# Decay exponents of a state-space scan built by differences between heads, and a root refinement moved to GpSimd

## The chip, the cores and the metric

The kernel runs on one core of a Trainium2 chip. The metric is the device time of one execution in microseconds. Before the change it is 1761.82 us, the median of 3 runs (1761.11 to 1761.87).

## The reference

Two transformer blocks over 512 positions of width 1024 are computed in float32. The change is in the second block's second mixer, a bidirectional state-space scan (`ssd_mixer`) with 32 heads of 64 channels in 4 groups of 8 heads, 4 chunks of 128 positions, and a state of 128. Cut to what matters:

```python
cs = jnp.cumsum(aa, axis=1)                          # log decay, per head
seg = cs[:, :, None] - cs[:, None, :]
decay = jnp.exp(jnp.where(mask, seg, -jnp.inf))      # 128 x 128 per chunk, head and direction
qk = jnp.einsum('bjgn,blgn->bjlg', qq, kk)           # shared by the 8 heads of a group
y_intra = jnp.einsum('bjlgh,blghp->bjghp', qk[..., None] * decay, vv)
...
y = y.reshape(bsz, s, SSD_INNER) * jax.nn.silu(z)
yg = y.reshape(bsz, s, SSD_GROUPS, SSD_INNER // SSD_GROUPS)
yg = yg * lax.rsqrt(jnp.mean(yg * yg, axis=-1, keepdims=True) + EPS)
```

## The kernel before, in words

Features lie on the partitions, positions along the free dimension. Large products are made in three passes of fp32r parts (`three`, L387 to L389: high by high, low by high, high by low). The weights come by DMA through a ring of five slots; ScalarE makes their high part (L342), VectorE the low part (L349).

The scan (`ssd_pe`, `ssd_act`, `ssd_dve`, `ssd_pool`) runs over four groups g of eight heads, and each engine's program is an order written out by hand, with semaphores between them. After a state part (`turn_x`, `states`, `between`), a group has 16 **steps** n, one for each head and direction. The four head pairs i of a group, the two heads hh of a pair and the two directions d make up n.

- `spread` on TensorE (L2309, L2310) fills one bank of PSUM (4 or 5, by n % 2) with two matmuls: the mask (`veil`, -1e30 where the mask is off) through the identity, and the running decay sums `cst_t` of one head, picked by a column of `sel` and broadcast to all rows. It waits until the exponentials of step n-2 have read the bank (`e_x`).
- `decays` on ScalarE (L2436) takes the exponential of the bank in four pieces of 128 columns, with a bias for each chunk, into one of four buffers `em`. It waits for `spread` (`xp`) and for the consumer of the buffer (`intra`).
- `weigh` on VectorE (L2582) multiplies the buffer by the products `gmat`, from SBUF into SBUF.
- `inside` on TensorE (L2327) multiplies two weighed buffers (both heads of the pair, one direction) into the output bank. There are eight of it in a group, m = 0 to 7, 16 matmuls of 128 columns each in pairs of column groups.
- `carried` (L2318) adds what comes from the states, once for each pair.
- `evac_y` on VectorE (L2587) takes the finished pair out of PSUM after steps 5, 9, 13 and after 15. GpSimd then gates it (L2514), from SBUF into SBUF.

Before the change, step n stands for pair n // 4, direction n % 4 // 2, head n % 2. So `inside` of index m reads steps 2m and 2m+1.

Between the steps TensorE does parts of the projection z (`part_z`, 6 matmuls of 512 columns a part). In the last group it has none, and does parts of the output projection instead (`out3_step`). ScalarE also does `gates` (two table loads and four Silu, L2442 to L2445), ahead of the steps in groups 0 to 2 and before step 4 in group 3, further the high part of a weight slot after step 8, the logarithm and exponential for the roots of group g-1 after step 1 (L2418, L2420). In group 3 it also makes high parts of the output (L2424).

VectorE finishes the roots of group g-1 in groups 1 to 3: `root_half` after step 4 (L2600), three refining operations after steps 5, 6 and 7 (L2605, L2608, L2612), and `normed_y` after steps 9 to 12 (L2616). After step 11 stand a low part of a weight slot and `take_z` (L349, L2570; not in group 3), and in group 3 low parts of the output (L2635).

The order on TensorE within a group is, for m = 0 to 7: `spread` of steps 2m+2 and 2m+3, `carried` if m is even, `part_z` if m is odd, `inside`. In group 3 come `out3_step` for the tiles k = 0, 1, 2 after m = 1 (18 matmuls) and more of them after m = 4 to 7.

Of the kernel before, what the change touches and what calls it, by code (L numbers as in the profile page):

```python
# [12 lines left out]
P = 128  # L13
D = 1024
S = 512
# [152 lines left out]
def build(nc, dr, ctx, start):  # L168
# [61 lines left out]
    vtl = at("vtl", [P, 2, GW], ST + 95)  # L230
    btok = at("btok", [P, TT, NS], ST + 99)
    nrm_a = at("nrm_a", [P, S], ST + 101)
    em = at("em", [P, 4, S], 56)
    sel = at("sel", [P, 2 * SH], 102.75, F32R)
    aneg = at("aneg", [P, 2 * SH], 102.5)
    cv = at("cv", [P, 4, S], ST + 8)
    cs_tmp = at("cs_tmp", [P, S], ST + 16, F32R)
# [1845 lines left out]
        return buf[:, :, :, :].rearrange("p c d h -> p (c d h)")  # L2083

    def step_of(n):
        return n // 4, n % 2, n % 4 // 2

    def swept(s, d):
        return s if d == 0 else TT - 1 - s
# [155 lines left out]
    def ssd_pe(pe):  # L2245
# [56 lines left out]
        def spread(g, n):  # L2302
            i, hh, d = step_of(n)
            if n < 2:
                pe.wait_ge(xtc, TT * (g + 1))
            else:
                pe.wait_ge(e_x, STEPS * g + n - 1)
            col = SH * d + HPG * g + 2 * i + hh
            nc.tensor.matmul(bank[4 + n % 2][:, :], ident_r[:, :], veil[:, d:d + 1, :].to_broadcast([P, TT, P]), start=True, stop=False)  # L2309
            nc.tensor.matmul(bank[4 + n % 2][:, :], sel[:, col:col + 1].to_broadcast([P, P]), cst_t[:, :], start=False, stop=True).then_inc(xp, 1)  # L2310

        def carried(g, i):
            if i < 2:
# [6 lines left out]

        def inside(g, m):
            i, d = m // 2, m % 2
            pe.wait_ge(mlu, STEPS * g + 2 * m + 2)
            for c in range(TT):
                for hh in range(2):
                    n = 2 * m + hh
                    mm = nc.tensor.matmul(bank[2 + i % 2][hh * HD:(hh + 1) * HD, c * P:(c + 1) * P],  # L2327
                                          xtok[:, c, (2 * i + hh) * HD:(2 * i + hh + 1) * HD], em[:, n % 4, c * P:(c + 1) * P],
                                          start=False, stop=d == 1 and c == TT - 1, skip_group_check=True)
            mm.then_inc(intra, 1)  # L2330

# [6 lines left out]
            for q in range(4):  # L2338
                part_z(t, q)
        pe.wait_ge(xsilu, 24)  # L2340
        pe.wait_ge(sel_done, 2)
        begin(0)
        for g in range(SG):
            turn_x(g)
            part_z(4 * g + 2, 0)
            states(g, 0)
            part_z(4 * g + 2, 1)
            part_z(4 * g + 2, 2)
            between(g, 0)
            part_z(4 * g + 2, 3)  # L2350
            states(g, 1)
            part_z(4 * g + 3, 0)
            part_z(4 * g + 3, 1)
            between(g, 1)
            part_z(4 * g + 3, 2)
            states(g, 2)
            part_z(4 * g + 3, 3)
            spread(g, 0)
            spread(g, 1)
            between(g, 2)  # L2360
            if g:
                norm_sum(g - 1)
            if g + 1 < SG:
                for q in range(4):
                    part_z(4 * g + 4, q)
            for m in range(8):
                if m < 7:
                    spread(g, 2 * m + 2)
                    spread(g, 2 * m + 3)
                else:  # L2370
                    if g + 1 < SG:
                        begin(g + 1)
                if m % 2 == 0:
                    carried(g, m // 2)
                if m % 2 and g + 1 < SG:
                    part_z(4 * g + 5, m // 2)
                inside(g, m)
                if g == SG - 1:
                    for k in ((), (0, 1, 2), (), (), (3,), (4,), (5, 6), (7,))[m]:
                        out3_step(pe, 0, k)  # L2380
                        out3_step(pe, 1, k)
# [44 lines left out]
    def ssd_act(act):  # L2426
        z0 = PLAN["z"]["slot0"]

        def decays(g, n):
            i, hh, d = step_of(n)  # L2430
            h = HPG * g + 2 * i + hh
            act.wait_ge(xp, STEPS * g + n + 1)
            if n >= 4:
                act.wait_ge(intra, 8 * g + n // 2 - 1)
            for c in range(TT):
                e = nc.scalar.activation(em[:, n % 4, c * P:(c + 1) * P], bank[4 + n % 2][:, c * P:(c + 1) * P], ACT.Exp,  # L2436
                                         bias=lbias[:, c, d, h:h + 1])
            e.then_inc(e_x, 1)

# [60 lines left out]
    def ssd_pool(pool):  # L2500
        pool.wait_ge(dt_ok, 1)
        pool.wait_ge(tri_load, 16)
        for d, m in enumerate(("gt", "le")):
            nc.gpsimd.tensor_scalar(veil[:, d, :], M[m], NEG, None, ALU.mult)
        nc.gpsimd.tensor_copy(ident_r[:, :], C["ident"]).then_inc(sel_done, 1)
        for g in range(SG):
            if g:
                for i in range(1, 4):
                    add_squares(pool, g - 1, i)
            for i in range(4):  # L2510
                k = 4 * g + i
                pool.wait_ge(yev, k + 1)
                pool.wait_ge(zs_done, k + 1)
                nc.gpsimd.tensor_tensor(xbc[:, k, :], xbc[:, k, :], zt[:, i, :], ALU.mult).then_inc(gated, 1)  # L2514
        for i in range(1, 4):
            add_squares(pool, SG - 1, i)

    def add_squares(pool, g, i):
        pool.wait_ge(ysq, 4 * g + i + 1)
# [4 lines left out]
    def ssd_dve(dve):  # L2524
# [53 lines left out]
        def weigh(g, n):  # L2578
            dve.wait_ge(e_x, STEPS * g + n + 1)
            if n == 0:  # L2580
                dve.wait_ge(gl_done, g + 1)
            nc.vector.tensor_tensor(em[:, n % 4, :], em[:, n % 4, :], gmat[:, :], ALU.mult).then_inc(mlu, 1)  # L2582

        def evac_y(g, i):
            k = 4 * g + i
# [12 lines left out]
        def root_half(g):  # L2598
            dve.wait_ge(yln, 2 * g + 1)
            nc.vector.tensor_scalar(nrm_a[:, :], bank[6][:, :], -0.5 / GW, -0.5 * EPS, ALU.mult, ALU.add).then_inc(yhalf, 1)  # L2600

        def root_first(g):
            dve.wait_ge(yhalf, g + 1)
            dve.wait_ge(yln, 2 * g + 2)
            link("dve", dve, nc.vector.tensor_tensor(xbc[:, C_TILE + g, :], nrm_a[:, :], xbc[:, B_TILE + g, :], ALU.mult))  # L2605

        def root_second(g):
            link("dve", dve, nc.vector.tensor_tensor(xbc[:, C_TILE + g, :], xbc[:, C_TILE + g, :], xbc[:, B_TILE + g, :], ALU.mult))  # L2608

        def root_third(g):  # L2610
            r = xbc[:, B_TILE + g, :]
            link("dve", dve, nc.vector.scalar_tensor_tensor(out=r, in0=xbc[:, C_TILE + g, :], scalar=1.5, in1=r, op0=ALU.add, op1=ALU.mult))  # L2612

        def normed_y(g, i):
            k = 4 * g + i
# [23 lines left out]
        for g in range(SG):  # L2639
# [13 lines left out]
            for n in range(STEPS):  # L2653
# [2 lines left out]
                    evac_y(g, n // 4 - 1)  # L2656
                if n == 4 and g:
                    root_half(g - 1)
                if n == 5 and g:
                    root_first(g - 1)  # L2660
                if n == 6 and g:
                    root_second(g - 1)
                if n == 7 and g:
                    root_third(g - 1)
                if 9 <= n < 13 and g:
                    normed_y(g - 1, n - 9)
                if n == 11 and g + 1 < SG:
# [48 lines left out]
    def _(pool):  # L2716
# [3 lines left out]
        nc.gpsimd.memset(half_eps[:, :], -0.5 * EPS).then_inc(set_done, 1)  # L2720
        pool.wait_ge(cst_load, 16)
        nc.gpsimd.tensor_tensor(sel[:, :], C["ident"][:, 0:2 * SH], C["ident"][:, 2 * SH:P], ALU.add).then_inc(sel_done, 1)
        one_pool(pool)
        two_pool(pool)
        up_pool(pool, 0)
# [243 lines left out]
```

## Time and profile before

| quantity | value |
|---|---|
| median of 3 runs | 1761.82 us |
| the profiled execution's own time | 1761.53 us |
| its span | 1759.8 us |
| TensorE (PE) busy | 1729.4 us, 98% |
| VectorE (DVE) busy | 1170.9 us, 67% |
| ScalarE (ACT) busy | 790.3 us, 45% |
| GpSimd (POOL) busy | 182.0 us, 10% |
| granted TensorE clock | 1.00 |
| the scan's steps | about 1092 to 1302 us |

Busy shares are of the whole span, and the scan is an eighth of it. In the timeline a row is one instruction or several merged: start, time from its start to its end, engine, line, operation, out<-in, how often. The bracket gives the idle time of the engine before it and what ended that. Ends overlap the next start, since the engines pipeline: the distance between starts is what an instruction occupies.

### The profile page before, as it was taken

How to read it: one execution, taken by the hardware profiler on the slowest of the kernel's cores; microseconds unless marked ns; L12 is line 12 of the kernel's file. 1: busy time of each engine (PE TensorE's matmuls, PEld its weight loads, DVE VectorE, ACT ScalarE, POOL GpSimd, SP SyncE). 2: the span in 40 equal slices, each digit the busy share in tenths (PEclk: the TensorE clock that was granted, in tenths of full speed). 3: DMA queues.
4: the chain of work that ended last, by engine and by line, in shares of the span. 5: the costliest groups of instructions: out<-in, count | busy, mean ns of one | idle time of the engine just before them, and what ended most of it. 6: DMA issues, size and time to landing. Idle time of an engine off the chain costs nothing.

```text
span 1759.8 us, 21732 instructions
## 1 busy us (share of the span) xinstructions
PE 1729.4 (98%) x8630; PEld 1380.5 (78%) x8630; DVE 1170.9 (67%) x1653; ACT 790.3 (45%) x1364; POOL 182.0 (10%) x203
## 2 busy tenths in 40 slices
PE   9999999999999999999999999999989999999998
PEld 7887877776578888888897886777668888888887
DVE  5565774867668887663368996766684688766334
ACT  5565652642244544442244544475562445444221
POOL 0421001400000111110000000221120001111000
PEclk9999999999999999999999999999999999999999
DMA  6211123311122222233323221011112132222332
GB/s 222 96 61 59 62 96 122 95 58 60 60 72 91 93 99 100 96 91 104 92 68 114 84 99 57 25 37 37 37 49 96 48 132 96 96 96 93 99 96 72
DMA packets 44277, 147.95 MB, mean 84 GB/s; under 512 B 5264, under 2 KB 8464, under 8 KB 44048
## 3 DMA queue, kind: packets, MB, share of 16 engines
q1 hardware_dynamic: 41728, 141.89, 24.3%
q10 hardware_dynamic: 2448, 4.66, 0.9%
q8 instruction: 69, 1.13, 0.3%
q14 instruction: 32, 0.26, 0.1%
HBM read 144.44 MB, written 2.10 MB: 83 GB/s over the span
## 4 chain that ended last, share of the span: by engine, by line
PE 82%; DVE 12%; ACT 4%; issue 1%; DMA 1%; POOL 1%; ACTq 0%; DVEq 0%; POOLq 0%
PE bank L387 21%; PE bank L389 21%; PE bank L388 21%; DVE cv L2226 4%; DVE w_lo L349 2%; PE bank L404 2%; PE bank L406 2%; PE bank L405 2%; PE bank L2327 1%; PE bank L2288 1%; PE bank L2300 1%; PE bank L983 1%; PE bank L996 1%; DVE bank L813 1%; PE bank L2309 1%
## 5 line engine op out<-in xcount | busy, mean ns | idle before, releaser
L387 PE MATMUL bank<-a_hi,w_hi 128*128 128x512 f32 x1384 | 555.2, 401 | 2.7 <-DVE a_lo L1270 1.1
L349 DVE TENSOR_TENSOR w_lo<-raw,w_hi 128x1024 fp32r<-128x1024 f32 (+1 forms) x257 | 328.2, 1282 | 335.6 <-ACT w_hi L342 335.0
L389 PE MATMUL bank<-a_hi,w_lo 128*128 128x512 f32 x1384 | 539.3, 390 | 0.0
L388 PE MATMUL bank<-a_lo,w_hi 128*128 128x512 f32 x1384 | 539.0, 389 | 0.0
L342 ACT ACTIVATE w_hi<-raw 128x1024 fp32r<-128x1024 f32 (+1 forms) x259 | 268.1, 1042 | 307.0 <-DMA raw<-in_w_down 143.5
L387 PEld LDWEIGHTS bank<-a_hi,w_hi 128*128 128x128 f32 x1384 | 259.8, 188 | 77.1 <-issue 20.3
L388 PEld LDWEIGHTS bank<-a_lo,w_hi 128*128 128x128 f32 x1384 | 259.9, 188 | 58.9 <-issue 6.9
L389 PEld LDWEIGHTS bank<-a_hi,w_lo 128*128 128x128 f32 x1384 | 259.8, 188 | 55.1
L1357 ACT ACTIVATE u<-bank,par 128x512 f32<-128x512 f32 x88 | 68.6, 779 | 177.8 <-DVE bank L813 177.8
L387 PE MATMUL bank<-g_hi,w_hi 128*128 128x512 f32 x308 | 119.8, 389 | 0.0
L388 PE MATMUL bank<-g_lo,w_hi 128*128 128x512 f32 x308 | 119.8, 389 | 0.0
L389 PE MATMUL bank<-g_hi,w_lo 128*128 128x512 f32 x308 | 119.8, 389 | 0.0
L1400 POOL TENSOR_TENSOR gv<-u 128x512 f32<-128x512 f32 x44 | 57.4, 1304 | 557.3 <-DVE u L1376 557.3
L2436 ACT ACTIVATE em<-bank,lbias 128x128 f32<-128x128 f32 x256 | 70.8, 392 | 33.7 <-PE bank L2310 33.4
L2582 DVE TENSOR_TENSOR em<-em,gmat 128x512 f32<-128x512 f32 x64 | 49.9, 787 | 38.6 <-ACT em L2436 38.4
L2226 DVE SCALAR_TENSOR_TENSOR cv<-bank,par,cv 128x510 f32<-128x510 f32 (+1 forms) x96 | 71.7, 747 | 2.5
L1376 DVE SCALAR_TENSOR_TENSOR u<-bank,par,u 128x511 f32<-128x511 f32 x88 | 66.0, 750 | 3.1
L389 PEld LDWEIGHTS bank<-g_hi,w_lo 128*128 128x128 f32 x308 | 57.8, 188 | 12.0
L388 PEld LDWEIGHTS bank<-g_lo,w_hi 128*128 128x128 f32 x308 | 57.8, 188 | 12.0
L387 PEld LDWEIGHTS bank<-g_hi,w_hi 128*128 128x128 f32 x308 | 57.8, 188 | 12.0
L404 PE MATMUL bank<-a_hi,w_hi 128*128 128x256 f32 (+1 forms) x192 | 61.1, 318 | 4.7 <-DVE w_lo L774 2.5
L1373 DVE SCALAR_TENSOR_TENSOR u<-bank,par,u 128x511 f32<-128x511 f32 x88 | 65.0, 739 | 0.0
(398 smaller groups left out, 2543.4 us busy)
## 6 DMA issues: line engine op xcount, KB each, us to landing
raw<-in_w_up SPq DMA_DIRECT2D x88, 512.0 KB, 3.2
raw<-in_w_in SPq DMA_DIRECT2D x50, 512.0 KB, 3.2
raw<-in_w_out SPq DMA_DIRECT2D x32, 512.0 KB, 3.7
raw<-in_w_down SPq DMA_DIRECT2D x32, 512.0 KB, 3.5
raw<-in_w_xbc SPq DMA_DIRECT2D x24, 512.0 KB, 3.2
raw<-in_w_z SPq DMA_DIRECT2D x16, 512.0 KB, 3.2
raw<-in_w_down SPq DMA_DIRECT2D x16, 384.0 KB, 3.1
raw<-in_w_mem_kv SPq DMA_DIRECT2D x4, 512.0 KB, 3.2
```

The source lines that it names most:

```text
L342: nc.scalar.activation(w_hi[:, q % RING, 0:w], raw[:, q % RING, 0:w], ACT.Copy).then_inc(hi_done, 1)
L349: nc.vector.tensor_tensor(w_lo[:, q % RING, 0:w], raw[:, q % RING, 0:w], w_hi[:, q % RING, 0:w].bitcast(F32), ALU.subtract).then_inc(lo_do ...
L387: nc.tensor.matmul(out, wh, rhs_hi[:, k, :], start=k == first, stop=False)
L388: nc.tensor.matmul(out, wh, rhs_lo[:, k, :], start=False, stop=False)
L389: return nc.tensor.matmul(out, wl, rhs_hi[:, k, :], start=False, stop=stop)
L404: nc.tensor.matmul(out, wh, rhs_hi[:, k, cols], start=start, stop=False, skip_group_check=True)
L1357: nc.scalar.activation(u[:, t % 4, :], tile_bank(name, t)[:, :], ACT.Identity, scale=pcol(f"ffn_w{layer}", 3 * t + 1), bias=pcol(f"ffn_b{l ...
L1373: nc.vector.scalar_tensor_tensor(out=ut[:, 1:S], in0=pt_[:, 0:S - 1], scalar=pcol(w, 3 * t), in1=ut[:, 1:S], op0=ALU.mult, op1=ALU.add).th ...
L1376: nc.vector.scalar_tensor_tensor(out=ut[:, 0:S - 1], in0=pt_[:, 1:S], scalar=pcol(w, 3 * t + 2), in1=ut[:, 0:S - 1], op0=ALU.mult, op1=ALU ...
L1400: nc.gpsimd.tensor_tensor(gv[:, i % 2, :], u[:, 2 * i % 4, :], u[:, 2 * i % 4 + 1, :], ALU.mult).then_inc(prod, 1)
L2226: nc.vector.scalar_tensor_tensor(out=dst, in0=tile_bank("xbc", tile)[:, a + by:b + by], scalar=pcol("conv_w", 5 * tile + tap), in1=dst, op ...
L2436: e = nc.scalar.activation(em[:, n % 4, c * P:(c + 1) * P], bank[4 + n % 2][:, c * P:(c + 1) * P], ACT.Exp, bias=lbias[:, c, d, h:h + 1])
```

## The change

It does two things. First, a step's exponents are made from those of the step before in the same bank. A bank belongs to one direction now. The mask is written once for each group and direction (n < 2), and each later step adds a matmul whose selecting column is the difference between this head's column and the preceding head's (`seld`), on top of what the bank holds. For this the steps are renumbered: pair n // 4, head n % 4 // 2, direction n % 2. `inside` of index m = 2i + d then reads steps 4i + d and 4i + 2 + d, there are five buffers `em` instead of four, and the order of TensorE is written anew. Second, the three refining operations leave VectorE for four on GpSimd, behind `add_squares` and ahead of the gating of the group's first pair. VectorE waits for them before `normed_y`, after step 9.

```diff
-    em = at("em", [P, 4, S], 56)
+    em = [at(f"em{n}", [P, S], kb) for n, kb in enumerate((56, 58, 60, 62, ST + 80))]
+    seld = at("seld", [P, 2 * SG, HPG], 103, F32R)
@@ step_of
-        return n // 4, n % 2, n % 4 // 2
+        return n // 4, n % 4 // 2, n % 2
@@ spread
-            col = SH * d + HPG * g + 2 * i + hh
-            nc.tensor.matmul(bank[4 + n % 2][:, :], ident_r[:, :], veil[:, d:d + 1, :].to_broadcast([P, TT, P]), start=True, stop=False)
-            nc.tensor.matmul(bank[4 + n % 2][:, :], sel[:, col:col + 1].to_broadcast([P, P]), cst_t[:, :], start=False, stop=True).then_inc(xp, 1)
+            if n < 2:
+                nc.tensor.matmul(bank[4 + d][:, :], ident_r[:, :], veil[:, d:d + 1, :].to_broadcast([P, TT, P]),
+                                 start=True, stop=False, skip_group_check=True)
+            nc.tensor.matmul(bank[4 + d][:, :], seld[:, SG * d + g, 2 * i + hh:2 * i + hh + 1].to_broadcast([P, P]), cst_t[:, :],
+                             start=False, stop=True, skip_group_check=True).then_inc(xp, 1)
@@ inside
-            pe.wait_ge(mlu, STEPS * g + 2 * m + 2)
+            pe.wait_ge(mlu, STEPS * g + 4 * i + 3 + d)
-                    n = 2 * m + hh
+                    n = 4 * i + 2 * hh + d
@@ the order of TensorE
+            spread(g, 2)
+            spread(g, 3)
+            carried(g, 0)
             for m in range(8):
-                if m < 7:
-                    spread(g, 2 * m + 2)
-                    spread(g, 2 * m + 3)
-                else:
-                    if g + 1 < SG:
-                        begin(g + 1)
-                if m % 2 == 0:
-                    carried(g, m // 2)
-                if m % 2 and g + 1 < SG:
-                    part_z(4 * g + 5, m // 2)
+                i, d = m // 2, m % 2
+                if m < 6:
+                    spread(g, 4 * i + 4 + 2 * d)
+                elif d and g + 1 < SG:
+                    begin(g + 1)
                 inside(g, m)
+                if m < 6:
+                    spread(g, 4 * i + 5 + 2 * d)
+                if d == 0 and g + 1 < SG:
+                    part_z(4 * g + 5, i)
+                if d and i < 3:
+                    carried(g, i + 1)
@@ decays
-            if n >= 4:
-                act.wait_ge(intra, 8 * g + n // 2 - 1)
+            if n >= 5:
+                act.wait_ge(intra, 8 * g + 2 * ((n - 5) // 4) + (n - 5) % 2 + 1)
@@ ssd_pool, in groups 1 to 3 after add_squares
+                refine_pool(pool, g - 1)
+    def refine_pool(pool, g):
+        a, r, t = nrm_a[:, :], xbc[:, B_TILE + g, :], xbc[:, C_TILE + g, :]
+        pool.wait_ge(yhalf, g + 1)
+        pool.wait_ge(yln, 2 * g + 2)
+        link("pool", pool, nc.gpsimd.tensor_tensor(t, a, r, ALU.mult))
+        link("pool", pool, nc.gpsimd.tensor_tensor(t, t, r, ALU.mult))
+        link("pool", pool, nc.gpsimd.tensor_scalar(t, t, 1.5, None, ALU.add))
+        link("pool", pool, nc.gpsimd.tensor_tensor(r, r, t, ALU.mult))
+        root_made.append(count["pool"])
@@ ssd_dve
-                if n == 5 and g:
-                    root_first(g - 1)
-                if n == 6 and g:
-                    root_second(g - 1)
-                if n == 7 and g:
-                    root_third(g - 1)
+                if n == 9 and g:
+                    dve.wait_ge(chain["pool"], root_made[g - 1])
@@ gpsimd, at the start of the program
+        pool.wait_ge(sel_done, 1)
+        heads_of = sel[:, :].rearrange("p (n h) -> p n h", h=HPG)
+        nc.gpsimd.tensor_copy(seld[:, :, 0:1], heads_of[:, :, 0:1])
+        nc.gpsimd.tensor_tensor(seld[:, :, 1:HPG], heads_of[:, :, 1:HPG].bitcast(F32), heads_of[:, :, 0:HPG - 1].bitcast(F32),
+                                ALU.subtract).then_inc(sel_done, 1)
```

## Rows read from the trace of the kernel before

**Rows 1.** The page: busy time of each engine, share of the span, instructions.

```profile
PE 1729.4 (98%) x8630; PEld 1380.5 (78%) x8630; DVE 1170.9 (67%) x1653; ACT 790.3 (45%) x1364; POOL 182.0 (10%) x203
```

**Rows 2.** Windows, steps of groups 0, 1, 3: PE, PEld, DVE, ACT, POOL busy, clock, DMA.

```profile
1096.00:1120.70 24.70, 24.70 (x214) 19.72 (x213) 14.33 (x19) 15.90 (x53) 3.82 (x3) 1.00 0.01 3
1153.80:1180.00 26.20, 25.16 (x216) 19.79 (x215) 19.49 (x28) 17.24 (x58) 5.63 (x3) 1.00 0.05 17
...
1266.60:1301.60 35.00, 29.07 (x221) 21.49 (x219) 27.19 (x37) 27.86 (x77) 6.87 (x3) 1.00 0.00 1
```

**Rows 3.** Timeline of TensorE in group 0.

```profile
1102.64 1.09 PE L2327 MATMUL bank<-em,xtok 128*64 128x128 f32 x16
1103.66 0.50 PE L2309 MATMUL bank<-veil,ident_r 128*128 128x512 f32 x1
1104.00 0.39 PE L2310 MATMUL bank<-cst_t,sel 128*128 128x512 f32 x1
1104.23 0.39 PE L2309 MATMUL bank<-veil,ident_r 128*128 128x512 f32 x1
...
1109.19 1.09 PE L2327 MATMUL bank<-em,xtok 128*64 128x128 f32 x16
```

**Rows 4.** Timeline of ScalarE, VectorE and GpSimd in group 0.

```profile
1107.94 2.17 ACT L2436 ACTIVATE em<-bank,lbias 128x128 f32<-128x128 f32 x8 [0.39 <-PE bank L2310]
1108.19 0.74 DVE L2587 SCALAR_TENSOR_TENSOR xbc<-xbc,par,bank 128x512 f32<-128x512 f32 x1
1109.01 1.27 POOL L2514 TENSOR_TENSOR xbc<-xbc,zt 128x512 f32<-128x512 f32 x1 [6.18 <-DVE xbc L2587]
1109.11 2.31 DVE L2582 TENSOR_TENSOR em<-em,gmat 128x512 f32<-128x512 f32 x2 [0.18 <-ACT em L2436]
```

**Rows 5.** Timeline in group 1, all engines.

```profile
1153.35 4.46 ACT L2436 ACTIVATE em<-bank,lbias 128x128 f32<-128x128 f32 x16
1153.85 1.09 PE L2327 MATMUL bank<-em,xtok 128*64 128x128 f32 x16
...
1157.43 0.68 DVE L2600 TENSOR_SCALAR nrm_a<-bank 128x512 f32<-128x512 f32 x1
...
1165.62 0.69 DVE L2582 TENSOR_TENSOR em<-em,gmat 128x512 f32<-128x512 f32 x1 [1.17 <-ACT em L2436]
...
1174.90 1.09 PE L2327 MATMUL bank<-em,xtok 128*64 128x128 f32 x16 [1.04 <-DVE em L2582]
1175.43 1.28 DVE L2582 TENSOR_TENSOR em<-em,gmat 128x512 f32<-128x512 f32 x2
```

**Rows 6.** Timeline in group 3, all engines.

```profile
1269.95 1.28 ACT L2442 ACT_TABLE_LOAD   x1
1270.19 1.09 PE L2327 MATMUL bank<-em,xtok 128*64 128x128 f32 x16
...
1274.75 1.14 ACT L2436 ACTIVATE em<-bank,lbias 128x128 f32<-128x128 f32 x4
...
1280.84 1.25 ACT L2436 ACTIVATE em<-bank,lbias 128x128 f32<-128x128 f32 x4
...
1286.55 0.68 DVE L2582 TENSOR_TENSOR em<-em,gmat 128x512 f32<-128x512 f32 x1
...
1296.53 2.88 POOL L2514 TENSOR_TENSOR xbc<-xbc,zt 128x512 f32<-128x512 f32 x1 [6.22 <-DVE xbc L2587]
1296.54 1.09 PE L2327 MATMUL bank<-em,xtok 128*64 128x128 f32 x16
1296.97 0.68 DVE L2582 TENSOR_TENSOR em<-em,gmat 128x512 f32<-128x512 f32 x1
```

**Rows 7.** Groups by line on GpSimd.

```profile
L2522 POOL TENSOR_TENSOR xbc<-xbc 128x512 f32<-128x512 f32 x12 | 15.4, 1284 | 14.9 <-ACT xbc L2414 14.9
L2504 POOL TENSOR_SCALAR veil<-tri 128x128 fp32r<-128x128 f32 x2 | 2.0, 985 | 171.9 <-DVE da L2162 171.8
L2718 POOL MEMSET spin<- 128x512 f32 x1 | 0.5, 524 | 0.0
```

More of the change, by code:

```diff
@@ L2322, in inside @@
             i, d = m // 2, m % 2
-            pe.wait_ge(mlu, STEPS * g + 2 * m + 2)
+            pe.wait_ge(mlu, STEPS * g + 4 * i + 3 + d)
             for c in range(TT):
                 for hh in range(2):
-                    n = 2 * m + hh
+                    n = 4 * i + 2 * hh + d
                     mm = nc.tensor.matmul(bank[2 + i % 2][hh * HD:(hh + 1) * HD, c * P:(c + 1) * P],
-                                          xtok[:, c, (2 * i + hh) * HD:(2 * i + hh + 1) * HD], em[:, n % 4, c * P:(c + 1) * P],
+                                          xtok[:, c, (2 * i + hh) * HD:(2 * i + hh + 1) * HD], em[n % 5][:, c * P:(c + 1) * P],
                                           start=False, stop=d == 1 and c == TT - 1, skip_group_check=True)
@@ L2340, in ssd_pe @@
         pe.wait_ge(xsilu, 24)
-        pe.wait_ge(sel_done, 2)
+        pe.wait_ge(sel_done, 3)
         begin(0)
@@ L2432, in decays @@
             act.wait_ge(xp, STEPS * g + n + 1)
-            if n >= 4:
-                act.wait_ge(intra, 8 * g + n // 2 - 1)
+            if n >= 5:
+                act.wait_ge(intra, 8 * g + 2 * ((n - 5) // 4) + (n - 5) % 2 + 1)
             for c in range(TT):
-                e = nc.scalar.activation(em[:, n % 4, c * P:(c + 1) * P], bank[4 + n % 2][:, c * P:(c + 1) * P], ACT.Exp,
+                e = nc.scalar.activation(em[n % 5][:, c * P:(c + 1) * P], bank[4 + n % 2][:, c * P:(c + 1) * P], ACT.Exp,
                                          bias=lbias[:, c, d, h:h + 1])
@@ L2516, in ssd_pool @@
             add_squares(pool, SG - 1, i)
+    root_made = []
+    def refine_pool(pool, g):
[7 more added lines that the diff above has]
+        root_made.append(count["pool"])
     def add_squares(pool, g, i):
@@ L2581, in weigh @@
                 dve.wait_ge(gl_done, g + 1)
-            nc.vector.tensor_tensor(em[:, n % 4, :], em[:, n % 4, :], gmat[:, :], ALU.mult).then_inc(mlu, 1)
+            nc.vector.tensor_tensor(em[n % 5][:, :], em[n % 5][:, :], gmat[:, :], ALU.mult).then_inc(mlu, 1)
         def evac_y(g, i):
@@ L2600, in root_half @@
             nc.vector.tensor_scalar(nrm_a[:, :], bank[6][:, :], -0.5 / GW, -0.5 * EPS, ALU.mult, ALU.add).then_inc(yhalf, 1)
[L2602 to L2612, printed above, removed]
         def normed_y(g, i):
```

## The prediction, made before the change was timed

> **What bounds the kernel now.** The busy times come first [rows 1]: TensorE is busy 98% of the span. A TensorE instruction taken away should then be worth its own time, wherever TensorE does not wait. The windows over the steps of the four groups say where that holds [rows 2]. In group 0 TensorE is busy all 24.7 us and no other engine over 16. In group 1 it is idle 1.0 of 26.2 us, with VectorE at 19.5 (group 2 is the same pattern once more, 59.1 us later). In group 3 it is idle 6 of 35 us, with VectorE and ScalarE at 27 to 28. So the gain is plain only in group 0. There the timeline [rows 3] shows what a matmul occupies: starts 0.23 us apart, though each lasts 0.39.
>
> An average doesn't show the dependences, so I then followed one pair of heads in the timelines of all engines. A step needs exponentials, 8 pieces in 2.17 us [rows 4], so 1.14 us until one step's are done and 1.03 between two; a weighing, 0.69 us [rows 5]; then `inside`, which occupies 1.02 us (from 1102.64 to 1103.66 [rows 3]). Before, `inside` m needs steps 2m and 2m+1, which are let go by `inside` m-2 or earlier, so spreads, `carried` or z hide this latency. A pair takes 6.55 us (from 1102.64 to 1109.19 [rows 3]), set by TensorE's order.
>
> **TensorE's gain.** Of 64 mask matmuls 8 stay. 56 x 0.23 = **12.9 us** less to issue, or 0.92 us a pair, half of what the spreads cost.
>
> **The new dependence.** `inside` of even index 2i+2 now needs step 4i+6 instead of 4i+5. That step's exponentials wait for `inside` 2i+1, which frees their buffer (five buffers: step 6 takes that of step 1). Before, nobody needed the step after it so soon. Set t = 0 at the end of `inside` 2i+1 and go on in group 0:
> - `evac_y` of the pair runs on VectorE to 0.8, and GpSimd starts gating at 0.85. Gating lasts 1.27 us, to 2.1.
> - The exponentials of step 4i+6 run from 0.1 to 1.25. The weighing is ready then but does not run: two weighings that began beside a gating took 2.31 us instead of 1.28 [rows 4, 5], so VectorE stood still until GpSimd was through. It runs from 2.1 to 2.8.
> - TensorE has only spread, `carried` and spread for this time, 1.4 us. It then idles 1.4 us until 2.8.
> - `inside`, spread, six z matmuls, spread with the small gaps after a wait, and the next `inside` add 1.02 + 0.23 + 1.38 + 0.30 + 1.02 = 3.95.
>
> The pair takes 2.8 + 3.95 = **6.75 us** and not 6.55: the latency costs more than the removed matmuls gave. Three such pairs add 0.6 to 0.9 us (0.85 with the ends of the waits), and the first `inside` starts 0.2 later, at the end of weighing 2. Group 0: **+1.0 us**.
>
> **Groups 1 and 2.** The first `inside` needs the weighing of step 2, whose exponentials start at 1153.35 behind the roots' logarithm and exponential [rows 5]. 1153.35 + 1.14 + 0.03 + 0.69 = 1155.2, against 1153.85 now: +1.4. The removed masks only pay this back. Two further terms count, both on VectorE:
> - **Refinement.** The three VectorE operations free 3 x 0.69 = 2.1 us, but GpSimd's four take the port from VectorE's weighings. A product takes GpSimd 1.28 us [rows 7]. For the 512-column scalar add the trace has no row: above it lies such a product (1.28), below it a memset of that size (0.52) [rows 7]. A scalar operation of a quarter of the columns took 0.985 us there, so I take 1.0. The block is 3 x 1.28 + 1.0 + links of 0.07 = 5.1 us. It starts at 1158.1, behind `root_half` (1157.43 + 0.68 [rows 5]); VectorE and GpSimd then alternate. Weighings 5, 6, 7 and 8 each wait for one operation of it. 1158.1 + 5.1 + 4 x 0.6 puts the end of weighing 8 at 1165.6. Then GpSimd gates the first pair, late, for 1.27. If it is first, weighing 9 starts at 1166.9, if VectorE is first, at 1165.6, where it starts now (1165.62 [rows 5]). A gating that lasted 2.88 us [rows 6] had been passed by more than one VectorE operation, so either occurs; nearer the upper end, since the gating then hits a later operation: **+1.0**.
> - **One weighing more.** From weighing 9 on VectorE is the bound: with evacuation, four normings, a weight's low part and z, it works without a gap from 1165.62 to the end of weighing 13, and `inside` 6 starts right behind that at 1174.90 [rows 5]. `inside` 6 now needs weighing 14, behind the evacuation at 0.66 and its own 0.6: +1.3.
>
> Together +2.3 a group, twice (group 2 repeats group 1). The block's own wait, before step 9's first norming, costs nothing: it ends before weighing 9. The sum for both is **+4.6 us**.
>
> GpSimd is said to be nearly as fast as VectorE for one-input elementwise work by the Trainium skill (GPSIMD Engine Reference, "Engine selection"); an estimate for the scalar add by that would be about 0.7 us, and each group then 0.3 us less. No row here has that operation at that size.
>
> **Group 3.** ScalarE does its gates ahead of step 4, 1269.95 to 1274.75 [rows 6]. Now TensorE fills that hole with `inside` 1 at 1270.19 [rows 6] and the 18 output matmuls right behind it. After the change `spread` 6, which waits for the exponentials of step 4 (1274.75 + 1.14 = 1275.9), stands **ahead of** `inside` 1. So `inside` 1, spread, `carried` and the 18 matmuls (1.02 + 0.3 + 0.95 + 4.14 = 6.4 us) start only at 1276.2 and end at 1282.6. Then comes `spread` 8, so step 8's exponentials start at 1283.1 and not at 1280.84 [rows 6]: +2.3. From there the chain of ScalarE and VectorE is as now, and weighing 9 moves from 1286.55 to 1288.85 [rows 6]. `inside` 6 again needs weighing 14, which now ends 1296.97 + 0.68 = 1297.65, 1.1 us behind the start of `inside` 6 at 1296.54 [rows 6]. That gives +3.4. Weighing 14 can also meet the gating of the third pair, 0 to +1.27, of which I take half: **+4.0 us**. What follows (gating, squares, sums, output projection) hangs on it and moves along.
>
> **The rest.** Two more GpSimd operations at the start (about 1 us each by [rows 7]) lie beside a time when nothing waits for GpSimd; were that cover gone they would cost 2 us. One z part moves from odd to even m, same length; no DMA is moved.
>
> **Sum.** 1.0 + 4.6 + 4.0 = +9.6 us. The profiled execution took 1761.5 us and its span 1759.8, so the next should have a span of about 1769.4 and a time of 1771.1. The median of the runs stands 0.3 us above the profiled execution: **1771.4 us**.
>
> **Rivals.**
> - *The saving comes through.* The mechanism is that the wait ahead of even `inside` stays below 0.92 us a pair, as it does if gating doesn't hold the weighing and GpSimd's refinement runs beside VectorE. For it: TensorE has no idle time in group 0 [rows 2]. Against: the 2.31 us [rows 4]. If all of it held, 1761.8 - 12.9 = 1748.9; with the latency alone (a pair of 1.25 + 0.7 + 3.95 = 5.9 instead of 6.55) and nothing of VectorE's bound, 9 pairs x 0.65 = 5.9 less: 1756.
> - *Even.* Gating and weighing collide in part only: group 0 gains 1.0, groups 1 and 2 stay, group 3 loses about 1.2 by `spread` 6. That is 1762.
> - *The port costs more.* Each GpSimd operation is lengthened by VectorE's as well, the scalar add takes 2 us, and normings then wait for the block. +2 us for each of three groups: 1777.4. For it: the gating of 2.88 us [rows 6].
> - *It doesn't do what it says.* Excluded for the matmuls, whose count is fixed in the code; if the roots came wrong nothing in time would change.
>
> The rule that decides between the first two is stated in the Trainium skill (SBUF — State Buffer, "SBUF: two separate sides"): VectorE operations with two SBUF inputs and GpSimd exclude each other for a whole instruction. By that rule, the trace agrees (2.31 us for two weighings).
>
> **How the numbers follow.** Forecast 0.70; the port costs more 0.08; even 0.09; the saving comes through 0.13. Its own range is 1767.5 to 1775: the scalar add (-1.4 to +0.8), the first gatings (-2 to +0.4), the gating in group 3 (0.6 either way), and a pair in group 0 between 6.5 and 6.9 us. For 8 in 10 I reach down toward even and up toward the dearer port: 1765.5 to 1777. A measurement tells about 0.2%, 3.5 us. Slower 0.79, same 0.09, faster 0.12.
>
> **What would show it.** In the profile after: mask matmuls x8; in groups 0 to 2, TensorE idle before even `inside`, ended by the weighing; weighings of 1.8 us or so next to GpSimd; in group 3 an idle stretch of about 5 us on TensorE before `spread` 6, and output matmuls only after 1277. If VectorE shows no long weighings, or the starts of `inside` in group 0 lie under 6 us apart by pairs, I am wrong.

## The result, and the profile after

| | median, us | lowest to highest | runs |
|---|---|---|---|
| before | 1761.59 | 1761.11 to 1761.87 | 4 |
| after | 1771.84 | 1770.33 to 1773.40 | 4 |

The ratio is 1.0059, 95% interval 1.0045 to 1.0073: the changed kernel is 10.2 us slower, though it issues 56 matmuls less. The page of the changed kernel, whose first lines answer to [rows 1]:

```profile
span 1770.4 us, 21612 instructions
## 1 busy us (share of the span) xinstructions
PE 1722.1 (97%) x8574; PEld 1373.8 (78%) x8574; DVE 1169.3 (66%) x1644; ACT 790.3 (45%) x1364; POOL 202.4 (11%) x217
```

TensorE is busy 7.3 us less over a span that is 10.6 us longer. So it stands idle 18 us more. Where that is, a table of one kind shows best, and it serves for all experiments: the time from the start of the last `inside` of one group to the start of the last of the next (for group 0 from the start of its first), in the one profiled execution of each kernel, minus the same time of the kernel before (23.60, 59.16, 59.13 and 62.58 us).

| kernel | group 0 | group 1 | group 2 | group 3 | median, us |
|---|---|---|---|---|---|
| after | +1.06 | +3.16 | +1.49 | +4.69 | 1771.84 |
| scan order alone | +1.08 | +1.81 | +1.86 | +4.84 | 1770.70 |
| roots on GpSimd alone | -0.01 | +0.43 | +0.41 | +1.30 | 1763.82 |
| six buffers | -2.53 | +0.82 | +0.83 | +3.97 | 1765.17 |
| gating set back | -1.09 | +2.83 | +1.48 | +4.69 | 1769.55 |
| order of group 3 | +1.05 | +1.48 | +1.52 | +3.69 | 1771.46 |
| six buffers, order of group 3, roots on VectorE | -2.53 | +1.78 | +1.80 | +1.14 | 1763.45 |
| the same, evacuation and normings later | -2.81 | -2.77 | -2.78 | +0.79 | **1753.92** |
| evacuation later alone | -1.11 | +2.36 | +2.46 | +3.74 | 1768.78 |
| before, evacuation and normings later | -0.01 | -0.97 | -0.50 | -0.01 | 1759.67 |
| fast one, roots on GpSimd | -2.81 | -2.16 | -2.13 | +1.72 | 1756.49 |
| fast one, five buffers | -1.09 | -0.95 | -0.91 | +0.78 | 1759.00 |
| fast one, the change's order in group 3 | -2.84 | -2.79 | -2.78 | +3.58 | 1756.66 |

In the change itself the four add up to 10.4 us, and the first `inside` of group 0 starts 0.2 later: that is the 10.6 us of the span. Counted from the group's first exponential, `inside` starts 3.98 us on instead of 3.78, so that 0.2 belongs to the new order too.

**Group 0.** The timeline of the changed kernel, all engines but the weight loads, to be held against [rows 3, 4]:

```profile
1100.47 0.75 DVE L2607 SCALAR_TENSOR_TENSOR xbc<-xbc,par,bank 128x512 f32<-128x512 f32 x1 [0.78 <-PE bank L2330]
1100.53 3.20 ACT L2443 ACTIVATE em<-bank,lbias 128x128 f32<-128x128 f32 x12 [1.57 <-PE bank L2330]
1101.30 1.27 POOL L2522 TENSOR_TENSOR xbc<-xbc,zt 128x512 f32<-128x512 f32 x1 [137.83 <-DVE xbc L2607]
1101.70 2.75 DVE L2602 TENSOR_TENSOR em<-em,gmat 128x512 f32<-128x512 f32 x3 [0.49 <-ACT em L2443]
1103.17 1.09 PE L2330 MATMUL bank<-em,xtok 128*64 128x128 f32 x16 [0.95 <-DVE em L2602]
...
1110.08 1.09 PE L2330 MATMUL bank<-em,xtok 128*64 128x128 f32 x16 [0.96 <-DVE em L2602]
```

`inside` 1 ends at 1100.4. All that was forecast follows from it in this order: exponentials of step 6 from 1100.53 (ScalarE waited 1.57 us for that `inside`), evacuation, gating at 1101.30, a weighing that is ready at 1101.70 and stands until about 1102.6, the end of the gating, `inside` 2 at 1103.17 behind it. A pair takes 6.91 us (1103.17 to 1110.08) and not 6.55.

**Group 3.** Two views of the changed kernel: the timeline of TensorE and ScalarE, against [rows 6], and windows (busy us of PE, PEld, DVE, ACT, POOL, each with its instructions, then granted clock, DMA share and GB/s):

```profile
1275.59 0.49 PE L2312 MATMUL bank<-cst_t,seld 128*128 128x512 f32 x1
1281.86 0.79 PE L2312 MATMUL bank<-cst_t,seld 128*128 128x512 f32 x1 [5.78 <-ACT em L2443]
1282.58 1.98 PE L2330 MATMUL bank<-em,xtok 128*64 128x128 f32 x16
...
1290.93 0.40 PE L2312 MATMUL bank<-cst_t,seld 128*128 128x512 f32 x1
1291.26 1.09 PE L2330 MATMUL bank<-em,xtok 128*64 128x128 f32 x16
1291.37 1.14 ACT L2443 ACTIVATE em<-bank,lbias 128x128 f32<-128x128 f32 x4 [3.49 <-PE bank L2312]
```

```profile
1166.00:1171.00 5.00, 2.92 (x28) 2.22 (x28) 5.00 (x5) 3.20 (x12) 2.92 (x2) 0.98 0.01 3
1171.00:1176.00 5.00, 5.00 (x34) 3.89 (x34) 5.00 (x8) 1.14 (x4) 0.00 (x0) 0.68 0.00 2
...
1278.00:1284.00 6.00, 2.14 (x15) 1.71 (x17) 1.91 (x3) 5.84 (x14) 0.79 (x1) 0.67 0.00 0
1284.00:1290.00 6.00, 6.00 (x29) 5.03 (x26) 3.25 (x4) 3.21 (x10) 5.67 (x5) 0.76 0.00 0
```

TensorE waits 5.78 us for the exponentials of step 4 with `inside` 1 and the output matmuls behind it in its queue. Then comes what was not forecast: `inside` 1 takes 1.98 us instead of 1.09. The windows say why. The granted clock averages 0.67 and 0.76 of full there, so part of it is at the lower level (1.2 instead of 2.4 GHz): it averages 1.00 from 1276 to 1280, 0.51 from 1280 to 1287 and 1.00 again from 1287 to 1291, and TensorE had been idle from 1276.1 to 1281.9. The same happens in group 1 behind a wait of 2.08 us, and not in group 2 behind one of 2.09 us:

```profile
1170.81 1.97 PE L2330 MATMUL bank<-em,xtok 128*64 128x128 f32 x16 [2.08 <-DVE em L2602]
...
1175.44 1.09 PE L2330 MATMUL bank<-em,xtok 128*64 128x128 f32 x16
...
1233.13 1.09 PE L2330 MATMUL bank<-em,xtok 128*64 128x128 f32 x16 [2.09 <-DVE em L2602]
...
1236.20 1.09 PE L2330 MATMUL bank<-em,xtok 128*64 128x128 f32 x16
```

### The profile page after: what moved, and what is told of

It is laid out like the page before. It is cut to its first block, busy times and chain, and to the rows that moved or that the text cites. A ratio compares the mean times of both kernels' runs of the same rounds, so it can differ in the third digit from the quotient of the medians.

```text
span 1770.4 us, 21612 instructions
## 1 busy us (share of the span) xinstructions
PE 1722.1 (97%) x8574; PEld 1373.8 (78%) x8574; DVE 1169.3 (66%) x1644; ACT 790.3 (45%) x1364; POOL 202.4 (11%) x217
## 3 DMA queue, kind: packets, MB, share of 16 engines
q8 instruction: 68, 1.11, 0.3%
## 4 chain that ended last, share of the span: by engine, by line
PE 79%; DVE 13%; ACT 6%; issue 1%; DMA 0%; POOL 0%; ACTq 0%; DVEq 0%
PE bank L388 21%; PE bank L389 20%; PE bank L390 20%; DVE cv L2227 4%; DVE w_lo L350 2%; PE bank L405 2%; PE bank L407 2%; PE bank L406 2%; ACT em L2443 1%; PE bank L2330 1%; DVE em L2602 1%; PE bank L2289 1%; PE bank L984 1%; PE bank L997 1%; PE bank L2301 1%
## 5 line engine op out<-in xcount | busy, mean ns | idle before, releaser
L2602 DVE TENSOR_TENSOR em<-em,gmat 128x512 f32<-128x512 f32 x64 | 54.1, 854 | 41.6 <-ACT em L2443 41.2
```

Source lines behind the costliest of these rows:

```text
L2602: nc.vector.tensor_tensor(em[n % 5][:, :], em[n % 5][:, :], gmat[:, :], ALU.mult).then_inc(mlu, 1)
```

## The experiments

In all of them the code is that of the changed kernel but for the edit shown, unless said otherwise.

### The scan order alone

```diff
@@ ssd_pool
-                refine_pool(pool, g - 1)
@@ ssd_dve: root_first, root_second, root_third back after steps 5, 6, 7
-                if n == 9 and g:
-                    dve.wait_ge(chain["pool"], root_made[g - 1])
```

> The new exponents and TensorE order alone; the roots' refinement stays on VectorE. Theory A (the step order costs most: the even inside waits for one step more, and group 3 waits for its gates): 1761.6 plus about 8 us, so 1768 to 1771, group 0 ends its last inside 1.3 us later as in the changed kernel, group 3 loses 3.5 to 4.5 us. Rival B (GpSimd's four operations and the port are the cost, and the saved matmuls are a gain): below 1760.

Measured: 1770.70 us (1769.86 to 1771.57), ratio 1.0053 (1.0038 to 1.0068). So the new order costs 9.2 us by itself, nearly all of it, and in group 3 even more than I gave it (4.84).

### The roots on GpSimd alone

The kernel before, with `refine_pool` and its wait put in, and the three operations of VectorE out.

> The kernel before with only the refinement moved to GpSimd. Theory A: a small loss, 1762 to 1766, with group 0 unchanged, weighings 5 to 8 of groups 1 to 3 lengthened by the GpSimd operations and weighing 9 of group 1 up to 1 us later. Rival B: most of the 10 us, 1768 or more. Rival C (VectorE is the bound and is relieved): 1756 to 1760.

Measured: 1763.82 us, ratio 1.0014 (1.0004 to 1.0023). A small loss of 2.3 us, 1.3 of it in group 3. The timelines of VectorE and GpSimd in group 1 of this kernel:

```profile
1160.43 2.20 DVE L2595 TENSOR_TENSOR em<-em,gmat 128x512 f32<-128x512 f32 x2 [1.08 <-ACT em L2436]
1163.47 1.43 DVE L2595 TENSOR_TENSOR em<-em,gmat 128x512 f32<-128x512 f32 x1 [0.83 <-ACT em L2436]
1165.45 1.14 DVE L2595 TENSOR_TENSOR em<-em,gmat 128x512 f32<-128x512 f32 x1 [0.55 <-ACT em L2436]
```

```profile
1158.06 1.67 POOL L2525 TENSOR_TENSOR xbc<-nrm_a,xbc 128x512 f32<-128x512 f32 x1 [26.10 <-DVE nrm_a L2613]
1159.80 1.27 POOL L2526 TENSOR_TENSOR xbc<-xbc 128x512 f32<-128x512 f32 x1
1161.16 1.82 POOL L2527 TENSOR_SCALAR xbc<-xbc 128x512 f32<-128x512 f32 x1
1163.06 1.29 POOL L2528 TENSOR_TENSOR xbc<-xbc 128x512 f32<-128x512 f32 x1
1164.43 1.61 POOL L2515 TENSOR_TENSOR xbc<-xbc,zt 128x512 f32<-128x512 f32 x1
```

Weighings are stretched where GpSimd's products lie (1.43 and 1.14 us instead of 0.69; the first row is two weighings, the second of them beside the scalar add, 1.09 us), and weighing 9 ends at 1166.59 instead of 1166.31 [rows 5] in a group that began 0.14 earlier: 0.4 us late, the group's whole loss. So the delays beside GpSimd take the place of the three operations that are gone from VectorE, and little more.

### Six buffers

```diff
-    em = [... enumerate((56, 58, 60, 62, ST + 80))]
+    em = [... enumerate((56, 58, 60, 62, ST + 80, ST + 91))]
-    ident_r = at("ident_r", [P, P], ST + 91, F32R)
+    ident_r = at("ident_r", [P, P], 102, F32R)
@@ decays (and n % 6 for n % 5 in decays, weigh and inside)
-            if n >= 5:
-                act.wait_ge(intra, 8 * g + 2 * ((n - 5) // 4) + (n - 5) % 2 + 1)
+            if n >= 6:
+                act.wait_ge(intra, 8 * g + 2 * ((n - 6) // 4) + (n - 6) % 2 + 1)
```

> The changed kernel with a sixth exponential buffer, so that step 4i+6 no longer waits for inside 2i+1 but for inside 2i. Theory A (latency loop over the buffer): in group 0 a pair falls from 6.9 us to about 5.7, group 0's last inside comes 2 us earlier than in the kernel before instead of 1.3 later; groups 1 and 2 stay bound by VectorE from weighing 9 on and gain little, group 3 nothing: about 1768. Rival (not the buffer but the gating on GpSimd holds the weighing in any case): group 0 stays at 6.9 us a pair and the time at 1771 to 1772.

Measured: 1765.17 us, ratio 1.0021 (1.0012 to 1.0031): 6.6 us won back. The timeline in group 0, all engines:

```profile
1099.81 0.75 DVE L2607 SCALAR_TENSOR_TENSOR xbc<-xbc,par,bank 128x512 f32<-128x512 f32 x1 [0.79 <-PE bank L2330]
1100.22 2.27 ACT L2443 ACTIVATE em<-bank,lbias 128x128 f32<-128x128 f32 x8 [0.30 <-PE bank L2312]
1100.47 0.69 DVE L2602 TENSOR_TENSOR em<-em,gmat 128x512 f32<-128x512 f32 x1
...
1101.24 1.09 PE L2330 MATMUL bank<-em,xtok 128*64 128x128 f32 x16
```

The weighing that `inside` 2 needs (at 1100.47) now starts right behind the evacuation and before the gating, because its exponentials no longer wait for `inside` 1. The pair takes 5.64 us, as forecast for this run. The sum was forecast too high (1768): in groups 1 and 2 a pass without the low clock loses 0.8 us instead of 1.5, where I had thought VectorE alone decided, and group 3 gained 0.7 where I had expected nothing. Group 1 of the table gains 2.3, because the changed kernel's profiled execution had the low clock there and this one had not.

### The gating set back

```diff
                 pool.wait_ge(zs_done, k + 1)
+                if i < 3:
+                    pool.wait_ge(mlu, STEPS * g + 4 * i + 7)
```

> The changed kernel with GpSimd's gating of pairs 0 to 2 waiting until step 4i+6 is weighed. Theory A (the gating takes the port just before the weighing that inside needs): a pair of group 0 falls from 6.9 to 6.0 us, group 0's last inside 0.7 to 1.5 us earlier than in the kernel before, 1768 to 1769.5 in all. Rival (the gating only lies beside it, the latency of exponentials and weighing alone sets the pair): 6.9 us a pair as before, 1771 to 1772.

Measured: 1769.55 us (1768.67 to 1774.88), ratio 1.0052 (1.0037 to 1.0067), at the upper end of what was expected. The pair of group 0 falls from 6.91 to 6.18 us, not to 6.0. So of the new loop 0.73 us a pair was GpSimd's gating ahead of the weighing, and 0.54 more (6.18 to 5.64) the wait of the exponentials for the buffer. Groups 1 to 3 move by 0.3 us at most. That in them VectorE works almost without gaps, so that only the place of the gating changes, is argued and not shown. Group 1 has the low clock in both profiled executions, here at `inside` 6 (1.98 us, behind a wait of 2.35).

### The order of group 3

In group 3 `inside` 1 and the 18 output matmuls go ahead of `spread` 6:

```diff
                 i, d = m // 2, m % 2
+                last = m == 1 and g == SG - 1
                 if m < 6:
-                    spread(g, 4 * i + 4 + 2 * d)
+                    if not last:
+                        spread(g, 4 * i + 4 + 2 * d)
 ...
                 inside(g, m)
+                if last:
+                    for k in range(3):
+                        out3_step(pe, 0, k)
+                        out3_step(pe, 1, k)
+                    spread(g, 6)
 ...
-                    for k in ((), (0, 1, 2), (), (), (3,), (4,), (5, 6), (7,))[m]:
+                    for k in ((), (), (), (), (3,), (4,), (5, 6), (7,))[m]:
```

> The changed kernel, in group 3 alone spread 6 and the 18 output matmuls set back: inside 1, the 18 matmuls, then spread 6, so that they fill the time of the gates. Theory A (the prediction's: the wait of spread 6 ahead of inside 1 costs 2.3 us of group 3's 4.7): about 1769.5, or 1768 with the low clock of that stretch gone too. Rival (in group 3 VectorE and GpSimd are the bound from step 8 on, with the extra weighing, and the idle stretch only moves): 1771 to 1772, inside 7 of group 3 at most 0.5 us earlier within its group.

Measured: 1771.46 us (1769.02 to 1773.46), which can't be told from the changed kernel; the profiled execution, the fastest of the four at 1769.02, has group 3 shorter by 1.0 us. By the time the rival holds, by the profile it is in between.

Up to group 3 this code is that of the changed kernel, so its trace also serves as a second one of groups 0 to 2. This execution had no low clock in group 1, and the group loses 1.48 us instead of 3.16, as group 2 does (1.51). So the low clock cost the changed kernel's profiled execution 1.7 us in group 1.

In group 3 TensorE's wait is not gone but comes later; timeline of VectorE and TensorE in this kernel, and a window with the columns as above:

```profile
1288.20 3.42 DVE L350 TENSOR_TENSOR w_lo<-raw,w_hi 128x1024 fp32r<-128x1024 f32 x2
...
1293.47 1.75 DVE L2609 TENSOR_TENSOR em<-em,gmat 128x512 f32<-128x512 f32 x1
...
1295.27 1.98 PE L2330 MATMUL bank<-em,xtok 128*64 128x128 f32 x16 [4.81 <-DVE em L2609]
```

```profile
1284.00:1295.00 11.00, 4.43 (x44) 3.34 (x44) 10.69 (x10) 8.51 (x26) 6.86 (x5) 1.00 0.01 1
```

VectorE is busy 10.7 of 11 us, and part of that is waiting beside GpSimd's 6.9: the two low parts take 3.42 us, in the changed kernel 2.35 (from 1293.75), the weighing 1.75 instead of 0.69. The output matmuls, done early, leave TensorE nothing for that time. It idles 4.81 us before `inside` 4, and the low clock follows.

### Six buffers, the order of group 3, and the roots on VectorE

The sixth buffer, the order of group 3, and the edit of the first experiment, which sets the roots back on VectorE, together.

> Six buffers, the order of the experiment before in group 3, and the refinement back on VectorE. Theory A (each part's cost adds): 3.5 from the buffer's 6.6 us and the roots' 1 to 2.5 off the changed kernel, group 3 another 1 to 3: 1761 to 1764. Rival (the parts cover each other, VectorE's order from weighing 9 sets the end in groups 1 to 3): 1764 to 1766.

Measured: 1763.45 us, ratio 1.0012 (1.0002 to 1.0021). Group 3 is down to +1.14, but groups 1 and 2 go from +0.8 with six buffers to +1.8: the roots on VectorE now stand ahead of weighing 6, which `inside` 2 needs. That what is left there is VectorE's order is a guess here, and the next experiment tests it.

### Evacuation and normings later: the fast one

On top of the last kernel:

```diff
-                if n in (5, 9, 13):
+                if n in (6, 10, 14):
                     evac_y(g, n // 4 - 1)
-                if 9 <= n < 13 and g:
+                if 9 <= n < 13 and g == SG - 1:
                     normed_y(g - 1, n - 9)
+                if n == 15 and 0 < g < SG - 1:
+                    for i in range(4):
+                        normed_y(g - 1, i)
```

> The experiment before, with evac_y of pairs 0 to 2 one weighing later (after steps 6, 10, 14), so that neither it nor GpSimd's gating stands ahead of the weighing that inside waits for, and with the four normings of groups 1 and 2 after weighing 15. Theory A (VectorE's order, not its load, holds TensorE; the removed masks are worth their time once it is mended): groups 0, 1 and 2 each 2 to 2.7 us shorter than in the kernel before, group 3 within 1 us of it: 1754 to 1757. Rival (VectorE's load is the bound): 1761 or more.

Measured: **1753.92 us** (1753.72 to 1754.26), ratio 0.9958 (0.9943 to 0.9973), 7.4 us faster than the kernel before, measured beside it (1761.32), and 18 us faster than the change. Groups 0 to 2 are each 2.8 us shorter. In group 0 this is the whole saving: 12 of its 14 lost mask matmuls stood behind the first `inside`, 12 x 0.23 = 2.8 us. In groups 1 and 2 all 14 are counted, 3.2 us. The longest waits of TensorE over all four groups (the view of waits, from 1090 to 1294 us; total, times, longest), in this kernel:

```profile
PE bank L2312 <- ACT em L2450: 7.5, 9, 1.6
PE bank L2330 <- DVE em L2608: 3.5, 6, 1.6
```

In the changed kernel, from 1090 to 1312 us, the same two lines are these (line numbers are each kernel's own):

```profile
PE bank L2330 <- DVE em L2602: 14.7, 14, 2.1
PE bank L2312 <- ACT em L2443: 11.1, 6, 5.8
```

In the kernel before, from 1090 to 1302 us:

```profile
PE bank L2327 <- DVE em L2582: 5.1, 5, 1.2
PE bank L2309 <- ACT em L2436: 3.1, 5, 0.8
```

So the fast one still waits 2.8 us more than the kernel before (11.0 against 8.2). Some of this is in group 3, which stays 0.8 us longer, and where the granted clock averages 0.57 from 1276 to 1280.

### Evacuation later alone

Only the first line of that edit, on the changed kernel.

> The changed kernel with evac_y one weighing later and nothing else. Theory A (evacuation and gating ahead of the critical weighing): 5 to 6 us less than the changed kernel, 1766 to 1767; group 0's pair near 6.0 us. Rival (only the gating counts): as with the gating set back, 1769.5.

Measured: 1768.78 us, ratio 1.0043 (1.0028 to 1.0058): 3 us, not 5 to 6. The rival (1769.5) was nearer. In group 0 it does what setting back the gating does (pair 6.19 us). Groups 1 and 2 lose 2.4 us each, more than group 2 of the change. In the profile `inside` 6 takes 1.85 and 1.98 us there, so it ran at the low clock, behind waits of 2.34 and 2.40 us; I take it that this takes back what VectorE gave, which no run here tests by itself.

### Four controls around the fast one

The kernel before with VectorE's new order alone (the last edit on the kernel before):

> Control: the kernel before with its masks and its four buffers, and only VectorE's order changed as in the fast experiment (evac_y after steps 6, 10, 14, the normings of groups 1 and 2 after weighing 15). Theory A (group 0 is bound by TensorE's instructions there, groups 1 and 2 lose only their 1 us of idle time): 1758.5 to 1760.5, group 0 unchanged. Rival (the whole gain of the fast experiment is VectorE's order and the removed masks give nothing): 1754.

The fast one with the roots on GpSimd:

> The fast experiment with the refinement on GpSimd as in the change. Theory A (the port costs more than VectorE is relieved): 2 to 7 us more than the fast experiment, 1756 to 1761. Rival (relief counts once the order is mended): 1753.9 or less.

The fast one with five buffers:

> The fast experiment with the change's five buffers instead of six. Theory A (the loop over the buffer costs 0.5 us a pair even without evacuation and gating in it): 3 to 5 us more, 1757 to 1759, group 0's pair 6.15 instead of 5.64 us. Rival (the sixth buffer doesn't matter once VectorE's order is mended): 1754.

The fast one with the change's own order in group 3:

> The fast experiment with the change's own order of TensorE in group 3 (spread 6 ahead of inside 1 and of the 18 output matmuls). Theory A (here VectorE leaves room, so the stretch counts, and the low clock after it too): 1755 to 1757. Rival (the idle stretch only moves, as it did in the changed kernel): 1754.

Measured against 1761.12 us: 1759.67 (0.9992, 0.9982 to 1.0001), 1756.49 (0.9975, 0.9965 to 0.9985), 1759.00 (0.9989, 0.9979 to 0.9998), 1756.66 (0.9975, 0.9965 to 0.9986). All four came out as the first theory said, the third at the edge of it. VectorE's order alone is worth 1.5 us, with an interval that just reaches no change, and group 0 does not move at all; the removed masks with the sixth buffer and the order of group 3 give the other 5.9 of 7.4. No run has the masks put back into the fast one, so in groups 1 to 3 these parts stay unseparated; in group 0, where TensorE had no idle time before, only fewer instructions could shorten it. Each against the kernel before that was measured beside it, the roots on GpSimd cost 2.8 us, the sixth buffer is worth 5.3, and the order of group 3 2.9, where in the changed kernel that order had been worth 1 us or less: a wait is worth mending only once the one behind it is.

## Why the prediction was right, and where its terms were off

The time (1771.4 forecast, 1771.84 measured) and the span (1769.4, 1770.4) were met, and the likeliest case was the one that happened. The signs that it named were there too: the pairs of 6.91 us, weighings of 1.8 us beside GpSimd, 5.8 us of idle TensorE before `spread` 6, and output matmuls only from 1286.6. The mechanism was right: one step more in front of every second `inside`, and in group 3 a `spread` that waits ahead of work that could run. That the number was met to 0.4 us was partly luck, since a term that was too large and one that was missing cancelled. By its steps:

- **The latency loop in group 0**: forecast 6.75 us a pair and +1.0 us, measured 6.91 and +1.28 with the later start of 0.22. Shown by two experiments that cut the loop at different places, the sixth buffer (5.64) and the later gating (6.18), and once more around the fast one (5.63 with six buffers, 6.19 with five).
- **One weighing more in groups 1 and 2** (+1.3): holds. In group 2, where the clock stayed full, `inside` 6 starts 9.84 us after the end of weighing 9, in the kernel before 8.58. The first `inside` starts 1.40 us later, as forecast. The whole loss is 1.49. This is VectorE and GpSimd there, timelines of the changed kernel:

```profile
1224.29 0.76 DVE L2602 TENSOR_TENSOR em<-em,gmat 128x512 f32<-128x512 f32 x1 [0.27 <-ACT em L2443]
1225.32 0.74 DVE L2602 TENSOR_TENSOR em<-em,gmat 128x512 f32<-128x512 f32 x1 [0.28 <-ACT em L2443]
1226.35 0.69 DVE L2602 TENSOR_TENSOR em<-em,gmat 128x512 f32<-128x512 f32 x1 [0.29 <-ACT em L2443]
1228.33 1.75 DVE L2602 TENSOR_TENSOR em<-em,gmat 128x512 f32<-128x512 f32 x1 [1.29 <-ACT em L2443]
...
1239.19 1.28 DVE L2602 TENSOR_TENSOR em<-em,gmat 128x512 f32<-128x512 f32 x2
```

```profile
1221.54 1.28 POOL L2532 TENSOR_TENSOR xbc<-nrm_a,xbc 128x512 f32<-128x512 f32 x1 [25.83 <-DVE nrm_a L2620]
1222.89 1.60 POOL L2533 TENSOR_TENSOR xbc<-xbc 128x512 f32<-128x512 f32 x1
1224.58 1.81 POOL L2534 TENSOR_SCALAR xbc<-xbc 128x512 f32<-128x512 f32 x1
1226.48 1.71 POOL L2535 TENSOR_TENSOR xbc<-xbc 128x512 f32<-128x512 f32 x1
1228.27 1.27 POOL L2522 TENSOR_TENSOR xbc<-xbc,zt 128x512 f32<-128x512 f32 x1
```

- **The refinement, +1.0 in groups 1 and 2**: this step was mis-sized. Weighing 9 ends 0.2 us later than in the kernel before, counted from the last `inside` of the group before, and not 1.0. Weighings 6, 7 and 8 (from 1224.29) last 0.76, 0.74 and 0.69: they hardly wait. Of 5 to 9 only 5 (1.79 us, from 1221.58) and 9 were held, 9 by the late gating. The refinement costs 0.4 us in each of these groups when it is alone, and the group with it is 0.4 us shorter than without it in the new order (1.49 against 1.86). My alternation of VectorE and GpSimd, one for one, was wrong in two ways: GpSimd gave way more often (its operations stretch to 1.6 to 1.8 us), and the scalar add held no weighing for its whole length.
- **Group 3, +4.0**: measured 4.69. Its largest piece, `spread` 6 ahead of `inside` 1, was there: 5.78 us of wait, exponentials of step 8 at 1291.37, which is 10.5 us later than in [rows 6], of which 5.9 belong to the groups before. That makes 4.6 and not 2.3, since from the start of `inside` 1 to `spread` 8 at 1290.9 pass 8.4 us, for which I had 6.4; the clock was low for about the first half of them. The half gating ahead of weighing 14 (0.6) did not come: VectorE passed that gating. But that this delay sets the end was only half right, as the fifth experiment shows: without it VectorE and GpSimd hold `inside` 4, and the group gains 1.0 us. It is worth 2.8 us only beside a relieved VectorE.
- **The clock**: not in the prediction at all. In group 1 `inside` 4 to `inside` 5 takes 4.63 us, in group 2, with the same work, 3.07: 1.6 us; the same code without the low clock loses 1.7 us less in group 1 (fifth experiment). Groups 1 and 2 together lost 4.65 us for 4.6 forecast, of which the refinement was 1.6 too large and the clock 1.7. So this part was met by luck.
- **The range**: its terms above the forecast (0.8, 0.4, 0.6 and 0.45 for three pairs of 6.9 us) add up to 1773.7 and not to 1775; those below (1.4, 2, 0.6 and 0.75) reach 1766.7 and not 1767.5. The measured time lies inside either.
- **The rivals**: *the saving comes through* was wrong for the change but not for its idea: once the loop and VectorE's order are mended, group 0 gets back all of its 2.8 us, and groups 1 and 2 get 2.8 each, of which 1.0 and 0.5 come from VectorE's order without the masks' removal. *The port costs more* had a scalar add of nearly the right length (2 us forecast, 1.81 measured), but not its effect: the block ends before weighing 9, and no norming waits for it. The rule on the port (the Trainium skill, SBUF — State Buffer, "SBUF: two separate sides") agrees with the trace for products (weighings of 1.75 us), and not for the scalar add: by it the weighing at 1225.32 would have stood until the add ended at 1226.39, and it ended at 1226.06. For that add the Trainium skill (GPSIMD Engine Reference, "Engine selection") had led to an estimate of 0.7 us; the traces have 1.81 or 1.82 at all 21 places in seven kernels that hold it, whatever VectorE did beside it.

## What to carry to other kernels

Take an instruction away from an engine that is 98% busy, and its time comes back only if what stands behind it in the new order is ready by then. Before removing work, name for each consumer the last producer it waits for, and what frees that producer's buffer: here one step more in front of every second `inside` made a loop of exponentials, weighing and `inside`, and cost more than the removed mask matmuls saved. Order VectorE's list by who waits: evacuations and normings that nobody waits for stood ahead of the weighing that TensorE did wait for, and to mend that was worth 1.5 us in the kernel before and 9.5 us in the new one, once the sixth buffer and the order of group 3 were mended (1763.45 to 1753.92).

## What the runs showed of the hardware

- A single-input scalar add on GpSimd (128x512, SBUF to SBUF) spans 1.81 us where a product beside it takes 1.27 when free, and a weighing that began inside it took 0.74 us instead of 0.69 (1225.32 in 1224.58 to 1226.39). Products held a weighing up to 1.79 us. It was so in groups 1 to 3. The add was not always without effect: with the roots alone on GpSimd, a weighing that began in it at 1161.54, right behind another, took 1.09 us. That too ended before the add did (1162.63 against 1162.98), and why it was longer stays open.
- GpSimd, when it has to wait for VectorE, isn't served next in every case. Timeline of GpSimd in group 3 of the changed kernel, the gating of the third pair:

```profile
1305.98 4.69 POOL L2522 TENSOR_TENSOR xbc<-xbc,zt 128x512 f32<-128x512 f32 x1 [6.22 <-DVE xbc L2607]
```

  An operation of 1.27 us took 4.69, while VectorE ran six operations without a gap; it ended at 1310.67, after VectorE's list had come to a wait (idle from 1309.5).
- The granted clock of TensorE fell after waits of 2.08 us (group 1) and 5.78 us (group 3), to averages of 0.68 from 1171 to 1176 and 0.67 from 1278 to 1284; in group 3 it fell within the wait. After a wait of 2.09 us in group 2 at the same place it did not fall. With six buffers, the order of group 3 and the roots on VectorE it averages 0.57 from 1270 to 1274, behind a wait of 1.65 us.
- The executions of the changed kernel spread over 3.1 us, those of the kernel before over 0.8. Their mean granted clocks go with it: 0.997 at 1770.33 us, 0.996 at 1771.54 and 1772.13, 0.995 at 1773.40; with the order of group 3 changed, 0.999 at 1769.02, 0.998 at 1770.81, 0.996 at 1772.11 and 1773.46. A mean that is a thousandth lower is 1.8 us of TensorE's time over 1770, the size of these steps, so it is likely that the clock makes this spread; no run holds the clock fixed to show it.
